# Two feed-forward norms as columns: root and reciprocal on one value per token, the rows spread by TensorE

## The reference, cut to what matters

```python
def rmsnorm(x, g):
    xf = x.astype(jnp.float32)
    y = xf * lax.rsqrt(jnp.mean(xf * xf, axis=-1, keepdims=True) + EPS)
    return (y * g.astype(jnp.float32)).astype(x.dtype)

def swiglu(x, w_gate, w_up, w_down):
    return (jax.nn.silu(x @ w_gate) * (x @ w_up)) @ w_down

x = x + 0.5 * swiglu(rmsnorm(x, p['g_ffn1']), p['w1_gate'], p['w1_up'], p['w1_down'])
...
x = x + 0.5 * swiglu(rmsnorm(x, p['g_ffn2']), p['w2_gate'], p['w2_up'], p['w2_down'])
```

## Time and profile before

| | us |
|---|---|
| three runs | 2224.31 to 2226.76, median 2226.09 |
| the profiled execution's own time | 2230.03 |
| its span, from the first to the last instruction | 2228.1 |
| TensorE busy in it | 2166.5 |
| VectorE busy | 1345.7 |
| ScalarE busy | 712.0 |
| GpSimd busy | 399.7 |

### The profile page before, as it was taken

How to read it: one execution, slowest core, us unless ns; L and a number is a source line. 1 busy time by engine, 2 the same in 40 slices (tenths; PEclk the granted TensorE clock), 3 DMA queues, 4 the chain that set the end, 5 groups by cost and what they waited for, 6 DMA issues and landing times. The chain is left out here.

```text
span 2228.1 us, 37795 instructions
## 1 busy us (share of the span) xinstructions
PE 2166.5 (97%) x15020; PEld 2016.9 (91%) x15020; DVE 1345.7 (60%) x2013; ACT 712.0 (32%) x1270; POOL 399.7 (18%) x427
## 2 busy tenths in 40 slices
PE   6899999999999999989999999999999999999998
PEld 5899999998989888878898887989999999989897
DVE  7966766664423678899526155368766766644234
ACT  6422322322212325547403034154223223222122
POOL 1000000000000256768535321520000000000003
PEclk9999999999999999999999999999999999999999
DMA  3212212116423221153411062312122122164222
GB/s 139 77 59 96 76 58 96 67 59 236 125 67 93 73 96 39 59 143 103 163 38 58 20 246 77 135 40 78 59 96 76 58 96 76 59 232 125 66 72 81
DMA packets 70864, 206.67 MB, mean 93 GB/s; under 512 B 9703, under 2 KB 31207, under 8 KB 63079
## 3 DMA queue, kind: packets, MB, share of 16 engines
q1 hardware_dynamic: 67808, 201.84, 26.7%
q10 hardware_dynamic: 2951, 3.35, 0.4%
HBM read 161.14 MB, written 41.23 MB: 91 GB/s over the span
## 5 line engine op out<-in xcount | busy, mean ns | idle before, releaser
L807 PE MATMUL ps<-act_hi,op_hi 128*128 128x272 f32 x1280 | 370.2, 289 | 10.2 <-ACT p L1528 9.6
L808 PE MATMUL ps<-act_lo,op_hi 128*128 128x272 f32 x1280 | 371.6, 290 | 0.0
L809 PE MATMUL ps<-act_hi,op_lo 128*128 128x272 f32 x1280 | 370.8, 290 | 0.0
L707 POOL TENSOR_TENSOR w_hi<-w_raw,ones 128x256 fp32r<-128x256 f32 x148 | 134.4, 908 | 1033.3 <-DMA w_raw<-in_w_plain 790.6
L807 PE MATMUL ps<-act_hi,w_hi 128*128 128x288 f32 (+1 forms) x864 | 290.4, 336 | 7.3 <-DVE act_lo L1981 2.0
L807 PE MATMUL ps<-hs_hi,dn_hi 128*128 128x288 f32 (+1 forms) x864 | 284.9, 330 | 1.3 <-DVE x L2161 1.1
L809 PE MATMUL ps<-act_hi,w_lo 128*128 128x288 f32 (+1 forms) x864 | 283.9, 329 | 0.0
L808 PE MATMUL ps<-hs_lo,dn_hi 128*128 128x288 f32 (+1 forms) x864 | 282.4, 327 | 0.0
L809 PE MATMUL ps<-hs_hi,dn_lo 128*128 128x288 f32 (+1 forms) x864 | 282.3, 327 | 0.0
L807 PE MATMUL ps<-t_hi,op_hi 128*128 128x272 f32 x960 | 277.2, 289 | 0.2 <-DVE hid_t L2002 0.2
L808 PE MATMUL ps<-t_lo,op_hi 128*128 128x272 f32 x960 | 277.1, 289 | 0.0
(11 more groups left out here) (332 smaller groups left out, 4215.1 us busy)
## 6 DMA issues: line engine op xcount, KB each, us to landing
raw_gu<-in_w_gu SPq DMA_DIRECT2D x40, 1024.0 KB, 5.1
w_raw<-in_w_plain SPq DMA_DIRECT2D x54, 512.0 KB, 3.6
dn_raw<-in_w_dn SPq DMA_DIRECT2D x44, 512.0 KB, 4.2
hid<-hid_o SPq DMA_DIRECT2D x40, 544.0 KB, 3.7
hr<-hid SPq DMA_DIRECT2D x88, 144.0 KB, 2.1
hr<-hid SPq DMA_DIRECT2D x44, 256.0 KB, 2.7
x<-x_keep SPq DMA_DIRECT2D x16, 544.0 KB, 5.1
ck_T<-in_ck SPq DMA_DIRECT2D x8, 1024.0 KB, 7.2
```

The costliest lines, as they stand in the source:

```text
L707: steps.done(pool.tensor_tensor(hi[:, r, :], raw[:, r, :], one, ALU.mult))
L807: pe.matmul(out, wh, ah, start=(first and n == 0), stop=False, skip_group_check=goes_on)
L808: pe.matmul(out, wh, al, start=False, stop=False, skip_group_check=goes_on)
L809: ins = pe.matmul(out, wl, ah, start=False, stop=end, skip_group_check=goes_on)
```

## The change

For both feed-forward norms the sums are made per token as columns: `acc` is the stationary operand and one column of ones moves, so 96 or 128 tokens come out as one column of PSUM; a chunk of 288 is three columns of 96, the chunk of 512 four of 128. Root and reciprocal then work on 96x3 or 128x4 values. TensorE spreads the result to 128 equal rows by a matmul of the column, broadcast, with the identity; ACT copies the rows from PSUM to `rstd`. `WIDTH` is (96, 128, 96), `COLUMNS` is (3, 4, 3). The identity is loaded by one more DMA in each layer.

```diff
+COL_BANK, ROW_BANKS = 6, (7, 6, 7)
...
+            sp.dma_start(n_id[:, :], t_in["ident"]).then_inc(n_tab, 16)
...
+            def sum_columns(key, c, adds):
+                w, at_ = WIDTH[c], CH[c][0]
+                pe.wait_ge(sq_used, SQ0[key] + adds)
+                if c and key == "ffn1":
+                    pe.wait_ge(rms_done, SUM0[key] + c)
+                for k in range(COLUMNS[c]):
+                    i = sum(COLUMNS[:c]) + k
+                    ins = pe.matmul(ps[0:w, COL_BANK, i:i + 1], acc[:, at_ + k * w:at_ + (k + 1) * w], ones[:, 0:1],
+                                    start=True, stop=True)
+                ins.then_inc(ssq_mm, 1)
+            def row(f, key, c):
+                w = WIDTH[c]
+                pe.wait_ge(rstd_done, SUM0[key] + c + 1)
...
+                for k in range(COLUMNS[c]):
+                    ins = pe.matmul(ps[:, ROW_BANKS[c], k * w:(k + 1) * w],
+                                    rms_col[c][0:w, k:k + 1].to_broadcast([w, P]), n_id[0:w, 0:w],
+                                    start=True, stop=True)
+                ins.then_inc(row_mm, 1)
...
                 for c in range(NC):
                     conv_gate(f, 1, c)
+                    after(NC + c)
...
-                if c == 1:
-                    sum_chunk("ffn1", CH, 0, KT)
-                if c == 2:
-                    sum_chunk("ffn1", CH, 1, 2 * KT)
-                    sum_chunk("ffn1", CH, 2, 3 * KT)
+                if i == 1:
+                    sum_columns("ffn1", 0, KT)
+                if i == 2:
+                    row(ffn["ffn1"], "ffn1", 0)
+                    sum_columns("ffn1", 1, 2 * KT)
+                if i == NC:
+                    sum_columns("ffn1", 2, 3 * KT)
+                if i > NC:
+                    row(ffn["ffn1"], "ffn1", i - NC)
+            def norm_ffn2(i):
+                if i == 0:
+                    for c in range(NC):
+                        sum_columns("ffn2", c, 2 * KT)
+                if i == 1:
+                    row(ffn["ffn2"], "ffn2", 0)
+                    row(ffn["ffn2"], "ffn2", 1)
+                if i == 2:
+                    row(ffn["ffn2"], "ffn2", 2)
```

In ScalarE's queue (`roots` takes the roots of a chunk's columns, `take_row` copies a chunk's rows from PSUM):

```diff
-            def ffn_layer(f, gain, kept=None):
+            def ffn_layer(f, key, gain, kept=None):
                 conv_hi(f, "up1")
+                if key == "ffn1":
+                    roots(key, [2])
+                else:
+                    take_row(f, key, 0)
+                    take_row(f, key, 1)
...
                 for c in range(NC):
                     gained(f, gain, range(2 * c, 2 * c + 2))
+                    if c and (c == 2 or key == "ffn1"):
+                        take_row(f, key, c)
                     silu(f, 0, c)
...
-            for c in range(NC):
-                chunk_squares(c)
-            rms("ffn1")
+            chunk_squares(0)
+            chunk_squares(1)
+            roots("ffn1", [0])
+            chunk_squares(2)
+            take_row(ffn["ffn1"], "ffn1", 0)
+            roots("ffn1", [1])
...
-            rms("ffn2")
+            roots("ffn2", range(NC))
```

In VectorE's queue:

```diff
             def ffn_layer(f, key):
-                for c in range(NC):
-                    inverse_rms(key, then=lambda c: gate_first(f, c), which=[c])
+                def normed(c):
+                    dve.wait_ge(ssq_ev, SUM0[key] + c + 1)
+                    gate_first(f, c)
+
+                normed(0)
                 conv_lo(f, "up1")
+                if key == "ffn1":
+                    inverse_columns(key, [2])
                 ffn_up(f, 0, 0)
                 dve.wait_ge(f["xg"], upto(f, "xg", KH))
                 moving_sum(f, 0, 0, 0, TH, 0, 0)
+                normed(1)
                 ffn_up(f, 0, 1)
+                normed(2)
                 dve.wait_ge(f["xg"], upto(f, "xg", KT))
...
+                if c == 1:
+                    inverse_columns("ffn1", [0])
             conv_lo(ffn["ffn1"], "gate1")
-            mean_squares("ffn1", D, which=[0, 1])
-            mean_squares("ffn1", D, which=[2])
+            inverse_columns("ffn1", [1])
...
-            plain_residual("co", PAIR_CO, "ffn2", "g_ffn2", lambda s: None,
-                           lambda: mean_squares("ffn2", D, which=[0, 1]))
-            mean_squares("ffn2", D, which=[2])
+            plain_residual("co", PAIR_CO, "ffn2", "g_ffn2", lambda s: None, lambda: None)
             conv_lo(ffn["ffn2"], "gate1")
+            inverse_columns("ffn2", range(NC))
```

More of the change, by code:

```diff
@@ L229, in build @@
         small = at("small", [P, NSM], C0 + 1440)
+        assert P <= 144
+        n_id = at("n_id", [P, P], C0 + 1440)
         ACC0 = P0 + 68608
@@ L486, in build @@
         x_pv_mm, x_o_ev, x_own = sem("x_pv_mm"), sem("x_o_ev"), sem("x_own")
+        n_tab = sem("n_tab")
         y_done, y_tab, eps_set, row_mm = sem("y_done"), sem("y_tab"), sem("eps_set"), sem("row_mm")
@@ L836, in sum_chunk @@
                   .then_inc(ssq_mm, 1)
+            def sum_columns(key, c, adds):
[11 more added lines that the diff above has]
+                pe.wait_ge(rstd_done, SUM0[key] + c + 1)
+                if c == 0:
+                    pe.wait_ge(n_tab, 16 * (f["n"] + 1))
+                if c == 1:
+                    pe.wait_ge(rms_done, SUM0[key] + NC)
+                if c == 2:
+                    pe.wait_ge(ssq_ev, SUM0[key] + 1)
+                for k in range(COLUMNS[c]):
[3 more added lines that the diff above has]
+                ins.then_inc(row_mm, 1)
             def conv_gate(f, t, c, feed=None):
@@ L1438, in _ @@
                       lambda c: pe.wait_ge(g_ev["co"], 6 + NC * (KT - 1) + c + 1),
-                      lambda c: sum_within("ffn2", c), down_last)
+                      norm_ffn2, down_last)
         @block.scalar
@@ L1460, in rms, with roots, take_row @@
                     act.activation(of[:, o:o + n], of[:, o:o + n], ACT.Sqrt).then_inc(rms_done, 1)
+            def roots(key, which):
+                for c in which:
+                    w, k, i = WIDTH[c], COLUMNS[c], sum(COLUMNS[:c])
+                    act.wait_ge(eps_set, 1)
+                    act.wait_ge(ssq_mm, SUM0[key] + (c + 1 if key == "ffn1" else NC))
+                    act.activation(rms_col[c][0:w, 0:k], ps[0:w, COL_BANK, i:i + k], ACT.Sqrt, bias=eps[0:w, :],
+                                   scale=1.0 / D).then_inc(rms_done, 1)
+            def take_row(f, key, c):
+                o, n = CH[c]
+                act.wait_ge(row_mm, f["n"] * NC + c + 1)
+                act.activation(rstd[:, o:o + n], ps[:, ROW_BANKS[c], 0:n], ACT.Copy).then_inc(ssq_ev, 1)
             def hi_parts(key, src, gain=None, ready=None, chunks=range(NC), tiles=range(KT)):
@@ L1833, in cat_tile @@
                 return mix[:, M_U + k, :] if k < LT else mix[:, M_Q + k - LT, :]
-            act.wait_ge(eps_set, 1)
+            act.wait_ge(eps_set, 2)
             act.wait_ge(asq_mm, NB + 1)
@@ L1913, in _ @@
             conv_hi(ffn["ffn2"], "gate1")
-            rms("ffn2")
+            roots("ffn2", range(NC))
             act.wait_ge(act_lo_done, SPLIT0["ffn2"] + NC * KT)
-            ffn_layer(ffn["ffn2"], "g_ffn2", 16 + 16 * KT)
+            ffn_layer(ffn["ffn2"], "ffn2", "g_ffn2", 16 + 16 * KT)
             def final_sqrt(c):
                 w, k = WIDTH[c], COLUMNS[c]
-                act.wait_ge(eps_set, 1)
+                act.wait_ge(eps_set, 2)
                 act.wait_ge(ssq_mm, SUM0["final"] + c + 1)
@@ L1972, in inverse_rms, with inverse_columns @@
                         then(c)
+            def inverse_columns(key, which):
+                for c in which:
+                    w, k = WIDTH[c], COLUMNS[c]
+                    dve.wait_ge(rms_done, SUM0[key] + c + 1)
+                    dve.reciprocal(rms_col[c][0:w, 0:k], rms_col[c][0:w, 0:k]).then_inc(rstd_done, 1)
             def lo_parts(key, src, gain=None, chunks=range(NC), tiles=range(KT)):
@@ L2275, in _ @@
             dve.memset(ones[:, :], 1.0).then_inc(ones_set, 1)
+            dve.memset(eps, EPS).then_inc(eps_set, 1)
             dve.wait_ge(cst_in, 16)
@@ L2752, in result @@
                 o, n = CH[c]
-                dve.wait_ge(row_mm, c + 1)
+                dve.wait_ge(row_mm, 2 * NC + c + 1)
                 dve.scalar_tensor_tensor(out=y[:, m, o:o + n], in0=ps[:, RSTD_BANK, 0:n], scalar=c_("g_final", m),
```

6 lines of the change are left out of this document (3 added, 3 removed).

## The result

The changed kernel takes 2237.03 us in the median of 6 runs (2231.96 to 2240.07), against 2226.43 us for the kernel before in the same session: ratio 1.0043, 95% interval 1.0032 to 1.0055, so 7 to 12 us slower. The forecast was 2229.7 us and the range ended at 2233.0: the sign of the sum was right, its size too small by about 7 us. The profiled execution of after stands at the median (own time 2236.91 us); that of before stood 3.6 us above its own, so the two profiled runs differ by 6.9 us only.

What follows compares the result with a forecast made beforehand. It took the order of ACT's queue, with its stops behind DVE, to bound each feed-forward layer's front. First layer 4.1 us later less 0.5 in the second gave 3.6 more: 2226.09 becomes 2229.7 us, range 2225.5 to 2233.0.

Steps and rivals of the forecast that it cites:

- 4.1 later: First layer: DVE's four differences start at 66.9 in place of 62.79 us, bounds 2.7 and 4.8 later.
- G: Start of ACT's first x tile times gain; forecast 51.15 in the first layer, 1491.25 in the second.
- the stretch from G to the four differences: Both layers: ACT's run of 11.5 us plus stops of 3.3 and 0.95, together 15.75 us.
- the stops: ACT waits for DVE's scaled gate at the second Silu, 3.3 us, and ahead of the third, 0.95 with handovers.
- The rival of longer handovers: Slower: six more handovers per layer each take 0.1 us more, +4.8 us, 2230.9; chance 0.30.
- about 6: First layer: TensorE's wait at step j = 2 stays about 6 us.
- I count nothing for it: Second layer: no gain counted from the clock staying up behind j = 2, as j = 6 waits for DVE anyway.
- the waits of 6.06 and 3.58 us cover that: Both layers: TensorE's 2.3 us of new work per layer is hidden by its waits at j = 2.
- The term of -0.5: Second layer: the four differences start 0.5 us earlier, 1507.0 against 1507.47; bounds 1.2 earlier and 0.6 later.
- the rule that was weighed ahead of time: Long pauses between matmul bursts halve TensorE's clock; by it alone the sum would be 2.4 us better.
- DVE's relief: Faster rival: ACT's stops don't bind and DVE's saved work counts, 11.2 us together, 2214.9; chance 0.10.
- the clock counted: Clock rival, second layer: lower level goes and TensorE's gain isn't lost at j = 6, 2227.3; chance 0.08.

Runs made afterwards that it cites:

- norm1_first: Against sums_apart: in both layers DVE scales the 512-column chunk's gate ahead of the first two differences, not behind them; 2229.00 us, ratio 1.0007.
- sum3_early: Against sums_apart: first layer's last-chunk sums moved ahead of gate 1's products, rows of chunks 1 and 2 one product earlier; 2228.68 us, ratio 1.0007.
- sums_apart: Against the changed kernel: second layer's one-column sums one product later, between chunk 1's gate and up products; 2234.68 us, ratio 1.0033.
- before_again: The kernel before, unchanged, run again against itself; 2227.59 us, ratio 1.0003.
- thin_before: Kernel before with ten extra one-column matmuls in the second layer, between the wait for the squares and the first wide sum; 2230.67 us, ratio 1.0022.
- three pairs of runs: With against without empty TensorE instructions: kernel before (0.13% slower), first-layer change alone (0.11% less), kernel with both handover edits and early gained tiles (0.12% less).
- l1_only: Against the changed kernel: change kept in the first layer only, second layer's rows of 128 equal roots put back; 2234.35 us, ratio 1.0033.
- pad_before: Kernel before with 144 already reached waits (72 empty instructions) at the start of TensorE's program; 2230.13 us, ratio 1.0013.
- pad_l1: Against l1_only: 368 already reached waits (184 empty instructions) added at the start of TensorE's program; 2235.56 us, ratio 1.0031.

## Why the prediction was right and wrong

**First layer: right.** The term was 4.1 later, the trace has 4.4. Of its parts, G was put at 51.15 and is 50.66 with a start 0.79 earlier; the stretch from G to the four differences was put at 15.75 and is 66.37 - 50.66 = 15.71; the stops were 3.3 and 0.95 with handovers, and ScalarE's idle parts of them are 2.63 and 0.53. The rival of longer handovers is therefore out. norm1_first and sum3_early show both halves of the sum, stops and late root, each by taking it away. TensorE's wait at j = 2 is 5.5 us, as "about 6" had it.

**Second layer: the step that failed** is "I count nothing for it" of the clock, together with "the waits of 6.06 and 3.58 us cover that" of TensorE's new work. Both looked at the clock behind j = 2 only. The new matmuls don't stand at j = 2; the sums stand behind a wait of 1.56 us, ahead of the gate products on which G depends, so a fall there isn't covered by anything. G was put at 1491.25 and is 1497.23, that is 1493.2 after the 4.03 us of a later entry: 2 us late, while the 15.75 behind it held again (1512.92 - 1497.23 = 15.69). The term of -0.5 was +3.0 in the trace of after. Of these 3.5 us 1.9 lie ahead of the four differences; the other 1.6 lie behind them, where the clock falls a second time, behind the longer wait at j = 6 (4.00 us at 0.57 lose 1.7). What the forecast used as evidence, that a stretch with 1.62 us of idle time kept its clock, held with wide matmuls behind the wait; with the one-column sums behind it the clock fell.

That sums_apart has just the -0.5 of the forecast is chance. Its differences come 2.0 us early, not 0.5, because the edit removes the wait of 1.56 us as well, and the second fall, behind j = 6, is still there and takes 1.5 back:

```profile
1546.00:1550.00 4.00, 3.68 (x17) 3.71 (x18) 3.97 (x7) 1.81 (x3) 0.00 (x0) 0.57 0.00 0
```

Here the rule that was weighed ahead of time has to be read with care. The Trainium skill (TensorE: Matmul & The Clock Gate, "Why this matters for your kernels") speaks of pauses between bursts of matmuls. The traces show that a pause with one kind of matmul behind it keeps the clock (1.62 us in before_again) and nearly the same pause with another kind loses it (1.68 us in thin_before, 1.56 in after); a rule on pauses alone would not have told these two apart, and the measurement decides.

**A term that was missing.** The forecast priced the new instructions for the DMA queue and for TensorE's time, and put the place of TensorE's code at nothing without naming it. By three pairs of runs that is 2 to 3 us of the 7 that l1_only lost; of the pairs only pad_before is clear of no change by itself, and barely. That an instruction packet on its way delays the load beside it is only argued: the late loads near 680 us all have one beside them, but so has a load that wasn't late, and no run changed the packet alone without moving the code. Why the keys at 1290 us come late is seen only as far as this.

**The sum, again:** 4.4 (first layer), 3.0 (second), 2 to 3 (the place of the code) is 9.4 to 10.4, against 7.1 to 12.2 by the interval. This adds figures of single traces to differences of medians, so it shows that the three terms are enough, not that each is exact. The three rivals of the forecast had no part in it: handovers were as counted, DVE's relief became idle time as said (2.70 us ahead of the four differences), and the clock counted, but with the opposite sign and elsewhere.

## What to carry to other kernels

Matmuls of one column look free and count as busy; ask what stands ahead of them, and put them between whole products rather than behind a wait. Before taking work off an engine that isn't waited for, write down who will now wait for whom in the queues that get the new steps: here moving one scaled gate per layer ahead of two differences was worth 0.26%, and taking 7.25 us of reciprocals per layer off DVE, by itself, nothing. And where a variant differs in instruction count ahead of long straight code, a difference of 0.1% can come from where its code lies: a run with empty instructions, in a place where the engine waits anyway, tells that.

## What was not expected of the hardware

- In the second layer a wait of 1.56 to 1.68 us with ten matmuls of one column behind it (2.30 us in after, 3.06 in thin_before) halved the granted clock in all three traces that have it; the same wait with wide ones, or the same matmuls without the wait, left it at 1.00.
- 72 empty instructions in a place where TensorE waits made the kernel 0.13% slower (0.02 to 0.23); in its trace two loads, some 670 and 1280 us later, came late.
- An empty semaphore instruction takes TensorE 0.109 us (184 of them some 20 us in pad_l1).
